# The opening of a hybrid Hyena / FNet / RG-LRU layer: parameter vector ahead of x in the load order, root multiplied into two pieces of x, three of eight normalised chunks on ScalarE

## The reference

```python
def rmsnorm(x, g):
    y = xf * lax.rsqrt(jnp.mean(xf * xf, axis=-1, keepdims=True) + EPS)
    return (y * g.astype(jnp.float32)).astype(x.dtype)

# in trunk_layer, for the context and for the latent tokens with their own conditioning
mod = jax.nn.silu(c) @ w_ada[l] + b_ada[l]
sh1, sc1, g1, sh2, sc2, g2 = jnp.split(mod[:, None, :].astype(dt), 6, axis=-1)
h = rmsnorm(x, n1) * (1 + sc1) + sh1
u = h @ w_in
```

## Time and profile before

| | us |
|---|---|
| median of 3 timed runs | 2621.64 (2621.34 to 2622.27) |
| the profiled execution, its own time | 2618.41 |
| its span | 2616.5 |
| mean clock granted to TensorE in it, share of full | 0.978 |
| busy: TensorE / its weight loads | 2477.3 / 2099.3 |
| busy: VectorE / ScalarE / GpSimd | 1447.0 / 623.4 / 688.2 |

### The profile page before, as it was taken

The page is one execution under the profiler, slowest core; times in us unless marked ns, Lnnn a source line. Parts: engine busy times, 40 slices in busy tenths (PEclk is TensorE's granted clock), DMA queues, the critical chain, the costliest instruction groups (busy, mean ns, idle before and its releaser), DMA issues. The chain is left out here.

```text
span 2616.5 us, 34805 instructions
## 1 busy us (share of the span) xinstructions
PE 2477.3 (95%) x13478; PEld 2099.3 (80%) x13478; DVE 1447.0 (55%) x2691; ACT 623.4 (24%) x887; POOL 688.2 (26%) x300
## 2 busy tenths in 40 slices
PE   4599999999997999999979989999999999999997
PEld 2488888867775888888868878888888888888886
DVE  5778786566585777776764383752233322332236
ACT  3423222565664222222220011310000000000004
POOL 1011111221212222322224452433134231432220
PEclk8799999999998999999989999999999999999999
DMA  7144443211115222322354242111011000111002
GB/s 297 48 172 156 166 161 117 82 40 61 60 40 190 99 99 98 116 98 98 118 204 148 66 166 82 49 33 46 19 48 48 32 32 32 48 40 40 24 24 81
DMA packets 53752, 234.24 MB, mean 90 GB/s; under 512 B 6131, under 2 KB 8755, under 8 KB 48068
## 3 DMA queue, kind: packets, MB, share of 16 engines
q1 hardware_dynamic: 53700, 233.54, 24.9%
HBM read 178.98 MB, written 54.53 MB: 89 GB/s over the span
## 5 line engine op out<-in xcount | busy, mean ns | idle before, releaser
L801 PE MATMUL ps<-h_hi,w_hi 128*128 128x512 f32 (+1 forms) x2112 | 760.3, 360 | 15.1 <-DVEq L1718 9.4
L803 PE MATMUL ps<-h_hi,w_lo 128*128 128x512 f32 (+1 forms) x2112 | 750.0, 355 | 0.0
L802 PE MATMUL ps<-h_lo,w_hi 128*128 128x512 f32 (+1 forms) x2112 | 750.0, 355 | 0.0
L759 POOL TENSOR_TENSOR w_hi<-w_raw,zero_col 128x1024 fp32r<-128x1024 f32 x96 | 205.5, 2140 | 1638.4 <-PE ps L803 1198.6
L801 PEld LDWEIGHTS ps<-h_hi,w_hi 128*128 128x128 f32 x2112 | 400.8, 190 | 77.0 <-DVEq L1718 9.8
L803 PEld LDWEIGHTS ps<-h_hi,w_lo 128*128 128x128 f32 x2112 | 400.4, 190 | 57.3
L802 PEld LDWEIGHTS ps<-h_lo,w_hi 128*128 128x128 f32 x2112 | 400.9, 190 | 56.5 <-issue 0.2
L2051 DVE TENSOR_TENSOR a<-sil,ps 128x512 f32<-128x512 f32 (+1 forms) x66 | 39.5, 599 | 504.1 <-PE ps L803 501.8
L762 POOL TENSOR_TENSOR w_lo<-w_raw,w_hi 128x1024 fp32r<-128x1024 f32 x96 | 262.3, 2732 | 7.5
L2074 DVE SCALAR_TENSOR_TENSOR x<-ps,mod,x 128x512 f32<-128x512 f32 (+1 forms) x264 | 172.3, 661 | 98.1 <-PE ps L803 97.5
L802 PE MATMUL ps<-h_lo,wf_hi 128*128 128x512 f32 (+1 forms) x624 | 224.3, 359 | 0.0
(11 more groups left out here) (276 smaller groups left out, 3500.3 us busy)
## 6 DMA issues: line engine op xcount, KB each, us to landing
w_raw<-in_weights SPq DMA_DIRECT2D x146, 512.0 KB, 3.9
ada_w<-in_w_ada SPq DMA_DIRECT2D x18, 1024.0 KB, 8.2
scratch_gate_s<-g_st SPq DMA_DIRECT2D x24, 640.0 KB, 3.3
side<-scratch_gate_s SPq DMA_DIRECT2D x24, 640.0 KB, 4.0
scratch_k_s<-kstage SPq DMA_DIRECT2D x8, 1536.0 KB, 6.6
hy_k<-scratch_k_s SPq DMA_DIRECT2D x8, 1536.0 KB, 8.7
scratch_hy_s<-hout SPq DMA_DIRECT2D x16, 640.0 KB, 3.2
ada_early<-in_w_ada SPq DMA_DIRECT2D x6, 1024.0 KB, 20.7
```

The source lines that it names most:

```text
L759: nc.gpsimd.tensor_tensor(hi[:], w_raw[slot % 2][:], zero_col[:].to_broadcast([P, D]), ALU.add).then_inc(pool_step, 1)
L801: mm(out, w_pair[0], x_pair[0], start=first, stop=False)
L802: mm(out, w_pair[0], x_pair[1], start=False, stop=False)
L803: return mm(out, w_pair[1], x_pair[0], start=False, stop=last)
```

## The change

`vec` is loaded ahead of chunk 0 of x. The eight chunks of piece 0 are multiplied by the root behind the second condition sum, and the eight of piece 1 behind the third; both banks are freed there. In pieces 0 and 1, u is then made straight from x by ScalarE for k = 1, 3 and 5, by VectorE for the others, and h_hi comes straight from x. ScalarE copies piece 2's root out of its bank into SBUF (`rstd_ctx`, in a buffer of squares that is no longer used), and VectorE reads it from there.

```diff
+U_BY_ACT = [n < 2 * KD and n % KD in (1, 3, 5) for n in range(3 * KD)]
+def u_made(n, by_act):
+    return U_BY_ACT[:n + 1].count(by_act)
...
+        rstd_ctx = x_sq[1][:, LAT:T]
...
+            sp.dma_start(vec[:], dr["vec"]).then_inc(vec_in, 16)
             sp.dma_start(x_in[:, 0, :], dr["x"][0]).then_inc(x_loaded[0], 16)
             sp.dma_start(cvec[:], dr["cvec"]).then_inc(cvec_in, 16)
             for k in range(1, KD):
                 sp.dma_start(x_in[:, k, :], dr["x"][k]).then_inc(x_loaded[k], 16)
-            sp.dma_start(vec[:], dr["vec"]).then_inc(vec_in, 16)
...
+            act.wait_ge(proj_done[2], 1)
+            fn(rstd_ctx, ps[2][:, 0:CTX], ACT.Copy).then_inc(proj_free[2], 1)
             act.wait_ge(norm_ready, 1)
             for p, (a, e, seq) in enumerate(PIECES):
                 for k in range(KD):
-                    if p == 0:
-                        if k % 2:
-                            if k >= 2:
-                                act.wait_ge(h_ready, k - 1)
-                            fn(u_t[k % 2][:, 0:e - a], x_in[:, k, a:e], ACT.Identity, bias=mod[:, k, seq:seq + 1],
-                               scale=norm_a[:, k, seq:seq + 1]).then_inc(u_act, 1)
+                    n = KD * p + k
+                    if U_BY_ACT[n]:
+                        if n >= 2:
+                            act.wait_ge(h_ready, n - 1)
+                        fn(u_t[n % 2][:, 0:e - a], x_in[:, k, a:e], ACT.Identity, bias=mod[:, k, seq:seq + 1],
+                           scale=norm_a[:, k, seq:seq + 1]).then_inc(u_act, 1)
+                    if p < 2:
                         fn(h_hi[:, k, a:e], x_in[:, k, a:e], ACT.Identity, bias=mod[:, k, seq:seq + 1],
                            scale=norm_a[:, k, seq:seq + 1]).then_inc(hi_ready, 1)
                     else:
-                        act.wait_ge(u_ready, KD * p + k + 1 - KD // 2)
+                        act.wait_ge(u_ready, u_made(n, False))
...
-                if r == 1:
-                    dve.wait_ge(proj_done[0], 1)
-                for k in ((), (0, 1, 2, 3), (4, 5, 6, 7), ())[r]:
-                    dve.wait_ge(x_loaded[k], 16)
-                    own.add(tt(x_in[:, k, 0:512], x_in[:, k, 0:512], ps[0], ALU.mult))
-                if r == 2:
+                if r in (1, 2):
+                    p = r - 1
+                    a, e, _ = PIECES[p]
+                    dve.wait_ge(proj_done[p], 1)
+                    for k in range(KD):
+                        dve.wait_ge(x_loaded[k], 16)
+                        own.add(tt(x_in[:, k, a:e], x_in[:, k, a:e], ps[p], ALU.mult))
                     own.settle()
-                    dve.sem_inc(proj_free[0], 1)
+                    dve.sem_inc(proj_free[p], 1)
...
-                        if p == 0 and k % 2 == 0:
+                        if p < 2 and not U_BY_ACT[n]:
                             ts(u_t[n % 2][:, 0:e - a], x_in[:, k, a:e], norm_a[:, k, seq:seq + 1],
                                mod[:, k, seq:seq + 1], ALU.mult, ALU.add).then_inc(u_ready, 1)
-                        elif p:
+                        elif p == 2:
                             if k == 0:
-                                dve.wait_ge(proj_done[p], 1)
-                            stt(u_t[n % 2][:, 0:e - a], x_in[:, k, a:e], norm_a[:, k, seq:seq + 1], ps[p][:, 0:e - a],
+                                dve.wait_ge(proj_free[2], 1)
+                            stt(u_t[n % 2][:, 0:e - a], x_in[:, k, a:e], norm_a[:, k, seq:seq + 1], rstd_ctx,
                                 ALU.mult, ALU.mult).then_inc(u_ready, 1)
-                            if k == KD - 1:
-                                dve.wait_ge(u_ready, n + 1 - KD // 2)
-                                dve.sem_inc(proj_free[p], 1)
                     if k:
...
                         dve.wait_ge(hi_ready, n)
-                        if p == 0:
+                        if p < 2:
                             tt(h_lo[:, k - 1, a:e], u_t[(n - 1) % 2][:, 0:e - a], h_hi[:, k - 1, a:e].bitcast(F32),
                                ALU.subtract).then_inc(h_ready, 1)
```

More of the change, by code:

```diff
@@ L1265, in _ @@
                     else:
-                        act.wait_ge(u_ready, KD * p + k + 1 - KD // 2)
-                        fn(h_hi[:, k, a:e], u_t[(KD * p + k) % 2][:, 0:e - a], ACT.Identity,
+                        act.wait_ge(u_ready, u_made(n, False))
+                        fn(h_hi[:, k, a:e], u_t[n % 2][:, 0:e - a], ACT.Identity,
                            bias=mod[:, k, seq:seq + 1]).then_inc(hi_ready, 1)
@@ L1707, in _ @@
                             dve.wait_ge(h_ready, n - 1)
-                        if p == 0 and k % 2 == 0:
+                        if p < 2 and not U_BY_ACT[n]:
                             ts(u_t[n % 2][:, 0:e - a], x_in[:, k, a:e], norm_a[:, k, seq:seq + 1],
                                mod[:, k, seq:seq + 1], ALU.mult, ALU.add).then_inc(u_ready, 1)
-                        elif p:
+                        elif p == 2:
                             if k == 0:
-                                dve.wait_ge(proj_done[p], 1)
-                            stt(u_t[n % 2][:, 0:e - a], x_in[:, k, a:e], norm_a[:, k, seq:seq + 1], ps[p][:, 0:e - a],
+                                dve.wait_ge(proj_free[2], 1)
+                            stt(u_t[n % 2][:, 0:e - a], x_in[:, k, a:e], norm_a[:, k, seq:seq + 1], rstd_ctx,
                                 ALU.mult, ALU.mult).then_inc(u_ready, 1)
-                            if k == KD - 1:
-                                dve.wait_ge(u_ready, n + 1 - KD // 2)
-                                dve.sem_inc(proj_free[p], 1)
                     if k:
-                        if p:
-                            dve.wait_ge(u_ready, n - KD // 2)
-                        elif k % 2:
-                            dve.wait_ge(u_ready, k // 2 + 1)
+                        if U_BY_ACT[n - 1]:
+                            dve.wait_ge(u_act, u_made(n - 1, True))
                         else:
-                            dve.wait_ge(u_act, k // 2)
+                            dve.wait_ge(u_ready, u_made(n - 1, False))
                         dve.wait_ge(hi_ready, n)
-                        if p == 0:
+                        if p < 2:
                             tt(h_lo[:, k - 1, a:e], u_t[(n - 1) % 2][:, 0:e - a], h_hi[:, k - 1, a:e].bitcast(F32),
```

## The result

The changed kernel took 2604.48 us at the median of five runs (2601.62 to 2608.55), beside 2621.34 us (2617.76 to 2622.27) for the kernel before. The ratio is 0.9939, with an interval of [0.9926, 0.9953]: 12.3 to 19.4 us less. The forecast was 2607.8 us in 2603 to 2612, a saving of 13.8 us, which is a ratio of 0.9947. Timed again beside 18 runs of the kernel before (median 2619.2 us), the same kernel took 2607.38 us (2603.44 to 2608.85), ratio 0.9949 [0.9935, 0.9962]. Over the eleven executions of it in this study the median is 2606.28 us, and they reach from 2601.62 to 2608.85 us: a spread of 7.2 us, where the forecast allowed 2 us to each side of a clock case.

The account below looks back on a forecast made before the run. TensorE bounds the long part, so only the opening, a chain across engines, could shorten. 10.7 us at the first h_hi plus 3.1 us in the norm stage make 13.8 us: 2621.64 us becomes 2607.8 us, range 2603 to 2612.

Parts of the forecast that it names:

- The mark and the rest: End of norm stage: the last h_lo, at 101.45 us before, comes 13.8 us earlier, and that shift reaches the end whole.
- The vector ahead of x: Opening: VectorE's stop until 20.65 us goes, x comes 0.5 us later, and the angle reduction starts 6.4 us earlier.
- The meeting with GpSimd: VectorE's pair and diagonal product end at 41.9 us, ahead of GpSimd's split; ScalarE's second row copy comes 10.8 us earlier.
- The exposed multiplies: Ahead of the fourth condition sum: eight piece 1 multiplies are not hidden, exposing about 1.5 us of added work.
- The norm stage: First h_hi to last h_lo: 3.1 us gained, 0.4 in piece 0, 2.7 in piece 1, none in piece 2.
- The freed bank: Norm stage: TensorE no longer waits 9.38 us for piece 1's bank, which by itself gives nothing.
- The high one: Opening with TensorE's clock high from 44 us on: norm starts at 58.8 us, 16.0 us gained, 2605.6 us; chance 0.22.
- The one between: Opening with TensorE's clock between high and low, the forecast itself: 13.8 us gained, 2607.8 us; chance 0.42.
- The low one: Opening with TensorE's clock low throughout: third sum stays at 56.3 us, 12.4 us gained, 2609.2 us; chance 0.2.
- The vector does not land early: Opening: the first 57 us stay as before, only 1.5 us gained, 2620.1 us, not measurable; chance 0.05.
- GpSimd meets the multiplies: VectorE's multiplies until 51 us are stretched up to 2.2 times beside GpSimd: 10 us gained, 2611.5 us; chance 0.06.
- Slower by the mean clock: Long part: from 0.006 less mean TensorE clock the gain is gone; at 0.968 the time is 2633 us; chance 0.03.

Follow-up runs that it names:

- e4: Kernel before with the first two weight tiles loaded behind the transform matrices, so GpSimd's split starts later; 2612.17 us, ratio 0.9975.
- e1: Kernel before with only the parameter vector's load moved ahead of x; 2606.66 us, ratio 0.9951.
- e2: Changed kernel with the parameter vector's load moved back behind x; 2616.53 us, ratio 0.9988.
- e5: Changed kernel with the root spread behind the first condition row and the multiplies behind the first and second condition sums; 2603.38 us, ratio 0.9938.

## Why the prediction held, step by step, and where its sizes were off

*The mark and the rest.* The last h_lo held as the measure. In twelve profiles of ten different kernels the rest of the span is 2514.6 to 2517.5 us, while the last h_lo moved over 20.7 us.

*The vector ahead of x.* Softplus was forecast for 14.2 us and came at 14.23, the angle reduction for 15.1 and came at 15.06. The delay of x by 0.5 us that stands in this sum is not borne out, though. The first profile seemed to show 0.65 us (12.82 for 12.17). But the eight profiles with the vector ahead start at 11.74 to 12.82 us, mean 12.20, and the four with it behind at 12.07 to 12.39, mean 12.18. The delay is below what the start varies by itself, and the step was right in the first profile by chance.

*The meeting with GpSimd.* Forecast and seen: 3.0, 1.5, ended at 41.9 (41.82) us, with the copy at 44.6 (44.57). e4 shows by itself that the 6.62 us were GpSimd's. The multiplies were forecast not to be stretched, and were not.

*The exposed multiplies.* Forecast 1.5 us; 1.8 us in the first profile, and 1.8 us as the difference to e1 from the second row copy on.

*The norm stage.* Forecast 29.7 to 26.6, seen 26.19. Piece 2 was to stay at 7.8 us and took 85.10 - 77.25 = 7.85 us, with the root in SBUF. The pair of products with it takes 0.88 us, and 0.86 us with the root in PSUM. The Trainium skill, VectorE: DVE Perf Modes, section on the TRN2 errata, would have the SBUF form 62 cycles shorter. The trace does not show it, and the prediction's choice to go by the rows was right. The 0.4 us that were missed lie in pieces 0 and 1, which took 9.43 us (to 68.34) and 8.91 us (to 77.25) where 9.6 and 9.2 were forecast. (In the sum for piece 1, the 4.3 us said to be for the last two chunks are for the last four: otherwise it does not add up to eight.)

*The freed bank.* Said to be worth nothing by itself. e2 agrees: all of its gain at the last h_lo is VectorE's 3.5 us less 0.5, and the rest of its span is not shorter.

*The clock, the term that was mis-sized.* The prediction had three cases. The high one was worked out exactly: third sum 52.7 (52.56), first h_hi 58.8 (58.91), and a profiled execution of 2618.4 - 16.0 = 2602.4 us against 2601.62. The one between, which was forecast with 0.42, appears in none of the three profiles of the changed kernel. The low one was put at 62.4 us for the first h_hi and is at 64.45 and 64.67 us. The step that failed is the start of TensorE's second row at 41.3 us: it was carried over from the profile of before, whose squares took 2.39 us, that is at the high clock. All three cases start from this 41.3 us, the low one too, though it was to be "low throughout". With a low clock the squares alone are 2.04 us longer (4.43 us), so the row starts at 43.27 us, and it takes 3.64 us in place of 3.23: the copy stands at 46.98 us, 2.4 us behind the 44.6 that was forecast for every case. That is also why the low case was put at 2618.4 - 12.4 = 2606.0 us for a profiled execution, and 2608.85 and 2608.38 us were measured. Behind the copy the low case is nearly as forecast: 4.66 us to the multiplies (4.64 taken), 11.3 us to the third sum (11.7 taken) and 5.4 us from third to fourth sum.

The forecast of 2607.8 us is near the median of the executions (2606.28 us), but no profile shows the case that it was worked out for, so part of the hit is luck: it lay between a case that was right and one that was put some 2.5 us too early. Four of the eleven executions (2603.44 to 2606.28 us) lie between the profiled ones. They may be openings of the middle kind, and no trace of them exists. Two of the eleven are below the range's end of 2603 us.

*The rivals.* "The vector does not land early" fell with softplus at 14.23 us, which waited for no load; the vector landed 6.2 us after its issue, for 12.1 before. "GpSimd meets the multiplies" fell with the two 4.87 us. "Slower by the mean clock" fell as well: 0.98 after and 0.978 before, and the rest of the span, all of the long part, is 2514.6 to 2516.4 us in the three profiles for 2515.05 before.

*What is open.* What decides whether the clock is up when the squares begin. The traces of the first and the second profile are the same up to there but for 0.52 us in the start. In before and in e2 the squares even start at the same 43.59 us, and take 2.39 us in one and 4.43 us in the other. Open too is whether e5's narrower spread is real.

## What to carry to other kernels

A small tensor that many things hang on belongs ahead of the large one: here its place cost the large load nothing that could be measured, and gave nearly the whole gain. Of the 10.8 us at the copy, 6.4 are the earlier start, and the other 4.4 come from taking VectorE out of GpSimd's way. When a stretch covers another engine's variable length, price the low and the high case of every piece of that engine behind the removed cover, not only of those that the profile happens to show at both. And look at more than one profile of a kernel whose opening has small matmuls, before a difference of a few microseconds is given a cause.

## What the runs showed of the hardware that was not expected

The same program ran its opening in two ways, 6.1 us apart from start to first h_hi (46.09 and 52.15 us), with nothing different in it but TensorE's clock. The Trainium skill, TensorE: Matmul & The Clock Gate, Part 1, says that the number of matmuls at the low clock differs between runs of one kernel; the three profiles agree, and show its price here to be 0.2% of the time.

A fall came without an idle stretch to speak of. In the first profile the clock was up for the squares and down for the row behind the turn, and from 29.05 us on TensorE had stood idle for no longer than the 0.41 us ahead of that turn. Windows of that trace; columns are the stretch, its length, busy time and count of PE, PEld, DVE, ACT and POOL, then the granted clock, the DMA share and GB/s:

```profile
40.40:43.80 3.40, 3.40 (x30) 2.02 (x33) 1.49 (x2) 0.00 (x0) 1.28 (x1) 0.52 1.09 451
...
44.00:57.00 13.00, 9.55 (x106) 5.77 (x96) 9.10 (x17) 4.73 (x6) 6.99 (x4) 1.00 0.60 252
```

TensorE was busy for all of the 3.4 us in which the mean was 0.52, near the lower of its two levels (1.2 and 2.4 GHz), with the end of the turn and then 32-column weights, and is back at full clock in the window from 44 us on (the turns there take 1.02 us). The same view of the second profile:

```profile
44.00:57.00 13.00, 11.33 (x74) 5.50 (x66) 5.04 (x9) 3.75 (x4) 7.63 (x4) 1.00 0.54 224
```

It shows 1.00 where the lengths above are those of the low clock (1.84, 4.61 us). In the traces of this study the column stands at full until its first fall, whatever the lengths say, so at the beginning of a trace it can't be trusted. The length of a piece that is known at both levels can.
